# Input projection of a hybrid SSD, attention and PEER layer: 12 of its 30 column chunks multiply in pairs of 512 and 256 columns

## The reference, cut to what matters

```python
xn = rmsnorm(h, norm1_g[i])
proj = xn @ w_in[i]                      # 2048 x (1024 z, 1536 xBC, 16 dt, 1024 q, 128 k, 128 v)
z, xbc, dt_raw, q, k, v = jnp.split(proj, list(IN_SPLITS), axis=-1)
xbc = jax.nn.silu(causal_depthwise_conv(xbc, conv_w[i], conv_b[i]))
...
y_ssd = rmsnorm(ssd_scan(...) * silu(z))
y_att = rmsnorm(swa_sink_attention(q, k, v, attn_sinks[i]))
h = h + concatenate([y_ssd, y_att]) @ w_out[i]
h = h + peer_ffn(rmsnorm(h, norm2_g[i]), ...)      # top-16 of 16384 experts for each of 8 heads
return rmsnorm(h, norm_f_g)
```

## Time and profile before

| | |
|---|---|
| median of 3 runs | 1712.38 us (1712.38 to 1712.72) |
| profiled execution: its time, its span | 1712.57 us, 1710.9 us |
| TensorE busy | 1699.4 us (99% of the span), 9725 matmuls |
| VectorE busy | 1336.6 us (78%) |
| ScalarE busy | 928.2 us (54%) |
| 200 to 210 us (q stage): TensorE, VectorE, ScalarE busy | 10.00, 8.64, 7.89 of 10 us |

### The profile page before, as it was taken

How to read it: one execution, slowest core, us unless ns; L and a number is a source line. 1 busy time by engine, 2 the same in 40 slices (tenths; PEclk the granted TensorE clock), 3 DMA queues, 4 the chain that set the end, 5 groups by cost and what they waited for, 6 DMA issues and landing times.

```text
span 1710.9 us, 26973 instructions
## 1 busy us (share of the span) xinstructions
PE 1699.4 (99%) x9725; PEld 1487.6 (87%) x9725; DVE 1336.6 (78%) x2125; ACT 928.2 (54%) x1593; POOL 547.1 (32%) x337
## 2 busy tenths in 40 slices
PE   9999999999999999999999999999999999999997
PEld 9999998988888888888888888888888888888886
DVE  7888889878999998555555666668878888888887
ACT  7546756544555554554454454465555555555556
POOL 0000000000017787777783000067545422222210
PEclk9999999999999999999999999999999999999999
DMA  7655568776668887778787888899999999999994
GB/s 275 223 196 165 183 198 272 230 240 214 203 197 197 193 197 194 194 198 198 195 192 217 261 266 263 269 364 348 361 340 357 362 364 350 370 359 358 368 335 157
DMA packets 186545, 445.74 MB, mean 261 GB/s; under 512 B 59360, under 2 KB 94448, under 8 KB 177776
## 3 DMA queue, kind: packets, MB, share of 16 engines
q1 hardware_dynamic: 146688, 372.94, 64.6%
q0 software_dynamic: 39504, 71.55, 15.8%
q10 hardware_dynamic: 288, 0.53, 0.1%
HBM read 423.79 MB, written 20.57 MB: 260 GB/s over the span
## 4 chain that ended last, share of the span: by engine, by line
PE 98%; DVE 1%; DMA 0%; issue 0%; ACT 0%; SPq 0%; DVEq 0%
PE ps L1903 23%; PE ps L1909 12%; PE ps L1889 8%; PE ps L2309 7%; PE ps L2311 7%; PE ps L2325 7%; PE ps L2323 7%; PE ps L2321 7%; PE ps L1887 4%; PE ps L1941 3%; PE ps L1942 2%; PE ps L1943 2%; PE ps L2215 2%; PE ps L2131 1%; PE ps L2133 1%; PE ps L2132 1%
## 5 line engine op out<-in xcount | busy, mean ns | idle before, releaser
L1031 DVE TENSOR_TENSOR low<-raw,high 128x1024 fp32r<-128x1024 f32 x376 | 457.9, 1222 | 74.7 <-ACT high L670 64.2
L670 ACT ACTIVATE high<-raw 128x1024 fp32r<-128x1024 f32 x376 | 393.2, 1051 | 53.3 <-PE ps L1943 32.3
L1903 PE MATMUL ps<-acts,high 128*128 128x512 f32 x1472 | 350.5, 390 | 0.0
L1903 PEld LDWEIGHTS ps<-acts,high 128*128 128x128 f32 x1472 | 272.6, 188 | 54.2
L663 ACT ACTIVATE high<-raw 128x1024 fp32r<-128x1024 f32 x172 | 182.5, 1062 | 170.7 <-PE ps L2325 166.6
L621 POOL DMA_INDIRECT big<-v_tab,half_sb x64 | 119.0, 1860 | 477.5 <-DVE big L1775 290.9
L1038 DVE TENSOR_TENSOR low<-raw,high 128x1024 fp32r<-128x1024 f32 x172 | 206.5, 1223 | 62.0 <-ACT high L663 60.8
L601 POOL DMA_INDIRECT gate_scratch<-gates_sb,cells_sb x128 | 214.1, 1673 | 68.8 <-issue 68.8
L929 ACT ACTIVATE side<-ps 128x256 f32<-128x256 f32 x128 | 49.1, 383 | 315.7 <-PE ps L1909 212.7
L1909 PEld LDWEIGHTS ps<-acts,low 128*128 128x128 f32 x1472 | 188.7, 191 | 7.2
L1909 PE MATMUL ps<-acts,low 128*128 128x256 f32 x1472 | 190.9, 283 | 0.0
(11 more groups left out here) (308 smaller groups left out, 3195.4 us busy)
## 6 DMA issues: line engine op xcount, KB each, us to landing
raw<-u_tab SPq DMA_DIRECT2D x256, 512.0 KB
raw<-v_tab SPq DMA_DIRECT2D x172, 512.0 KB
raw_more<-v_tab SPq DMA_DIRECT2D x84, 512.0 KB
raw<-w_in SPq DMA_DIRECT2D x60, 512.0 KB
raw<-w_out SPq DMA_DIRECT2D x32, 512.0 KB
raw<-w_q SPq DMA_DIRECT2D x32, 512.0 KB
gate_scratch<-side SPq DMA_DIRECT2D x32, 384.0 KB, 5.7
big<-gate_scratch SPq DMA_DIRECT2D x16, 768.0 KB, 7.1
```

Source lines behind the costliest of these rows:

```text
L670: nc.scalar.activation(slot(high, s), slot(raw, s), ACT.Copy).then_inc(hi_done, 1)
L1031: V.tensor_tensor(slot(low, s), slot(raw, s), slot(high, s).bitcast(F32), ALU.subtract).then_inc(lo_done, 1)
L1903: mm(both, tile_of(high, kk), both_of(kk), start=(kk == 0), stop=False, skip_group_check=True)
```

## The change

Twelve chunks go over to matmuls in pairs: convolution chunks 10 and 11, keys, values, and the eight of q. Other than `paired_product`, the new `half_pairs` does the eight 512-column matmuls and the eight 256-column ones of one half chunk before it goes to the other half. The takes of these chunks become two VectorE operations with a wait between them: a product of 512 columns out of the bank into a new tile `in_two`, and the sum of its halves. `IN_PAIRED` names chunks 12 and 13 too, which `take_chunk` handles in its other branch.

```diff
+            def take_two(c, bank, dst, r):
+                two = in_two.rearrange("p (s n) -> p s n", s=2)
+                dve.wait_ge(taken, c)
+                dve.wait_ge(used, 2 * c + 2)
+                own.step(V.tensor_tensor(two, ps[:, bank, :].rearrange("p (s n) -> p s n", s=2),
+                                         r.rearrange("p (o n) -> p o n", o=1).broadcast_to([P, 2, T]), ALU.mult))
+                own.settle()
+                V.tensor_tensor(dst, in_two[:, 0:T], in_two[:, T:2 * T], ALU.add).then_inc(taken, 1)
...
+                    if c in IN_PAIRED:
+                        take_two(c, c % 2, conv_in[:, m, CONV_W - 1:CONV_W - 1 + T], rstd1)
+                        return
...
-                    take(c, c % 2, k_t if c == C_K else v_t, rstd1)
+                    take_two(c, c % 2, k_t if c == C_K else v_t, rstd1)
...
-                take(c - 1, (c - 1) % 2, view(QZ + s * T, T), rstd1)
+                take_two(c - 1, (c - 1) % 2, view(QZ + s * T, T), rstd1)
...
+            def half_pairs(c, half, first, last):
+                par = c % 2
+                s = 2 * par + half
+                for k in range(8):
+                    wh = high[:, s * PIECE + k * P:s * PIECE + (k + 1) * P]
+                    mm(ps[:, par, :], wh, both_tiles(8 * half + k), start=first and k == 0, stop=False, skip_group_check=True)
+                for k in range(8):
+                    wl = low[:, s * PIECE + k * P:s * PIECE + (k + 1) * P]
+                    ins = mm(ps[:, par, 0:T], wl, hi_tile(8 * half + k), start=False, stop=last and k == 7,
+                             skip_group_check=True)
+                return ins
+
+            def product_pairs(c):
+                pe.wait_ge(taken, c - 1)
+                for half in range(2):
+                    pe.wait_ge(lo_done, 2 * c + half + 1)
+                    half_pairs(c, half, half == 0, half == 1).then_inc(used, 1)
...
-            product(10, 0)
-            product(11, 1)
-            product(C_K, C_K % 2)
+            product_pairs(10)
+            product_pairs(11)
+            product_pairs(C_K)
...
-            product(C_V, C_V % 2)
+            product_pairs(C_V)
...
-            product(C_Q, C_Q % 2)
+            product_pairs(C_Q)
...
-                part(c, 0, every, acc, normed, True, False).then_inc(used, 1)
+                half_pairs(c, 0, True, False).then_inc(used, 1)
...
-                part(c, 1, every, acc, normed, False, True).then_inc(used, 1)
+                half_pairs(c, 1, False, True).then_inc(used, 1)
```

More of the change, by code:

```diff
@@ L52 @@
 C_WQ = C_OUT + KT
+IN_PAIRED = (10, 11, 12, 13)
 C_U = C_WQ + 2 * PEER_HEADS
@@ L155, in build @@
         sb(ctx, "unused", 2 * KT * T - 2 * DENSE - SPARSE - KT * DENSE - D - 2 * PIECE)
+        with ExitStack() as inputs:
+            in_two = sb(inputs, "in_two", 2 * T)
         with ExitStack() as routing:
@@ L2149, in spread @@
                 ins.then_inc(rows_ok, 1)
-            product(C_Q, C_Q % 2)
+            product_pairs(C_Q)
             pe.wait_ge(y_out, SSD_HEADS)
-            normed, mixed = (hi_tile, lo_tile), (plain(act2_hi), plain(act2_lo))
+            mixed = (plain(act2_hi), plain(act2_lo))
             every = range(8)
@@ L2156, in _ @@
                 c = C_Q + 1 + s
-                acc = ps[:, c % 2, 0:T]
                 pe.wait_ge(taken, c - 1)
                 pe.wait_ge(lo_done, 2 * c + 1)
-                part(c, 0, every, acc, normed, True, False).then_inc(used, 1)
+                half_pairs(c, 0, True, False).then_inc(used, 1)
                 if s:
```

## The result

The changed kernel took **1715.01 us** (median of 20 runs, 1713.76 to 1716.99), the kernel before 1712.58 us beside it (20 runs, 1712.15 to 1714.39): ratio 1.0014, 95% interval 1.0008 to 1.002. So it is 2.4 us slower, less than the 0.2% within which this kernel counts as unchanged, but the interval excludes 1. The forecast was 1715.3, +2.9. The profiled execution is the slowest of the 20 (1716.99 us, span 1715.4).

What follows compares the result with a forecast made beforehand. TensorE fills 98% of the chain, but the q-stage loop through VectorE's longer take was to bind: +0.31 us by chunk 15, growing to +2.9 at the last turn, on the 1712.38 median 1715.3 us, range 1712.6 to 1717.2.

Steps and rivals of the forecast that it cites:

- What TensorE saves: Twelve paired chunks: a half chunk falls from 2.88 to 2.78 us, 2.4 us at most over 24 halves.
- What VectorE pays: Each two-operation take: 0.68 product, 0.03 wait and 0.42 sum replace 0.42, so 0.71 us more.
- Chunks 10 to 13: Convolution, keys and values: takes of 10, 11 and 13 fall in idle time, take 12 does not; TensorE 0.31 us late.
- The stall ahead of chunk 15: TensorE waits 0.95 us for VectorE's low cut, 0.71 late, with the load ahead of it assumed unmoved.
- The restart: TensorE resuming after a wait in mid-stream at chunk 15: costs between nothing and 0.28 us, taken as 0.10.
- The q stage: Loop of logits, maxes, exponentials, shares, take: slack 0.49 to 0.56 us against 0.71 more per take; last turn +2.82, plus 0.04 restart.
- The steps that the forecast called covered, 2 and 4: q stage: longer takes there hidden behind other VectorE work, so no TensorE idle before logits.
- (A): Rival, whole kernel: VectorE's extra stays hidden and the whole 2.4 us is saved, 1710.0 us; chance 5%.
- (B): Rival: only the stall at chunk 15 comes and the q stage keeps its pace, -1.3, 1711.1 us; chance 8%.
- (C): Rival: measurably slower, from 0.78 us extra a take (+3.4) or restarts 0.10 dearer each; chance 27%.

Runs made afterwards that it cites:

- Pairs with the old take: Changed kernel with all pairs on TensorE, but VectorE's one-operation take of the left half, right half left out; -1.93 us against the kernel before, ratio interval 0.9983 to 1.0001.
- second profile of the changed kernel: Profile from running the changed kernel again without edit; that run's median was 1714.84 us against 1712.82 for the kernel before.
- best version: Changed kernel with q takes ahead of shares, keys' take earlier, add_halves of step 0 and a low cut of step 2 behind shares; 1710.98 us against 1712.54.
- the take ahead of shares: Changed kernel with take_two moved from behind shares to ahead of them in each q step; 1712.26 us against 1712.61 for the kernel before.

## Why the prediction was right, point by point

**What TensorE saves.** Right in kind, a little too high in size. A half fell from 2.88 to 2.80 us instead of 2.78, since eight wide matmuls take 1.84 us, 0.230 each and not the 0.228 of the earlier trace rows: 0.083 a half, 2.0 us for 24, not 2.4. Pairs with the old take gave -1.93. The Trainium skill ("TensorE: Matmul & The Clock Gate", Back-to-back issue gap) would have had 0.5 us in all by the formula that the forecast took, 109 and 216 ns; measured are 120 and 230 ns from start to start. The forecast left out that the section gives this formula for an isolated matmul and says that it under-counts at small N and over-counts at large N where each matmul follows a weight load of its own. Here the trace agrees with the first (120 for 109) and not with the second (230 for 216).

**What VectorE pays.** 0.684 + 0.04 + 0.425 - 0.42 = 0.73, forecast 0.71.

**Chunks 10 to 13.** Their takes are covered, as forecast. The stall ahead of chunk 15 is the term with a wrong premise: I held the landing of the load fixed, and it moves by 2.7 us from one execution to the next. TensorE's idle time there was 0.49 in the second profile of the changed kernel, and none is listed in the first (0.06 by the starts), 0.95 forecast. Counted from `cumulate`, chunk 15 started +0.28 late in the second profile (102.05 - 69.37 = 32.68 against 32.40), nearly the +0.21 of the forecast. The idle time is shorter for the same lateness for two reasons. 0.16 more is not listed, since the matmul of 101.28 is shown to 101.56 and the next was due at 101.40: by the starts the wait is 0.65. And TensorE had already waited once before, which the forecast missed: chunk 14 needs the bank that take 12 frees. In the second profile that take ends at 95.06 + 0.43 = 95.49 (VectorE):

```profile
94.35 0.68 DVE L1149 TENSOR_TENSOR in_two<-ps,big 128x512 f32<-128x512 f32 x1
95.06 0.43 DVE L1152 TENSOR_TENSOR big<-in_two 128x256 f32<-128x256 f32 x1
```

and TensorE, whose last eight narrow matmuls from 94.39 need 0.96, goes on at 95.54 and not at 95.35, with 0.23 to the second matmul in place of 0.12, so it loses 0.19 + 0.11 there. With the 0.65 that is 0.95, the forecast's sum, at two places in place of one; less 8 halves of 0.083 it is the +0.28.

```profile
94.39 1.11 PE L1939 MATMUL ps<-acts,low 128*128 128x256 f32 x8
95.54 0.39 PE L1978 MATMUL ps<-acts,high 128*128 128x256 f32 x1
95.77 0.28 PE L1979 MATMUL ps<-acts,high 128*128 128x256 f32 x1
```

In the first profile, with the load 0.9 earlier, that take is done in time, and chunk 15 starts 103.66 - 71.86 = 31.80 from `cumulate`, 0.60 early. The restart cost about what I took: 0.07 more at chunk 15 (0.19 from the first to the second matmul where 0.12 is usual) and 0.11 at chunk 14, against 0.10.

**The q stage.** The forecast shifts against those of the second profile, each less its `cumulate` (0.16 later than before):

| place | forecast | measured |
|---|---|---|
| logits(0) | 0.0 | +0.10 |
| logits(1) | +0.59 | +0.56 |
| logits(3) | +0.83 | +0.73 |
| logits(5) | +1.13 | +1.00 |
| last turn | +2.86 | +2.78 |

The takes between agree as well: the one of step 6 ended +2.04 for +2.11, that of step 7 +2.77 for +2.82. The steps that the forecast called covered, 2 and 4, are the two without a wait; the other five stall 0.39 to 0.41 each. The steps from logits to logits show the two kinds side by side (us):

| step | 0 | 1 | 2 | 3 | 4 | 5 | 6 | 7 (to the last turn) |
|---|---|---|---|---|---|---|---|---|
| before | 7.18 | 8.87 | 7.18 | 8.67 | 7.78 | 7.78 | 8.14 | 6.89 |
| changed, second profile | 7.64 | 8.74 | 7.48 | 8.52 | 8.20 | 8.31 | 8.67 | 7.61 |
| moved takes, best version | 7.16 | 8.73 | 7.03 | 8.85 | 7.74 | 7.64 | 8.07 | 6.89 |

The long steps 1 and 3 fell by 0.13 to 0.15, TensorE's saving; in every other step the loop through VectorE is the longer and the step grew by 0.30 to 0.72. The best version pays in step 3 alone (+0.18, the late turn above) and gains in the rest or stays level. From logits(0) to the last turn the changed kernel needs 65.11 us in the first profile and 65.17 in the second, before 62.49, the best version 62.11.

**Against the rivals.** That the extra stays hidden (A) or that only chunk 15 stalls (B) is ruled out by the run with q only: +2.64, with the same waits in the q stage. The measurable loss (C) did not come: it needed 0.78 more per take or dearer restarts, and 0.73 a take and 0.07 to 0.11 a restart were measured.

**What stays less certain.** The median moved by +2.0 to +2.4, the shift from `cumulate` to the last turn by +2.78 in one profile and +1.85 in the other; these two differ by the stall at chunk 15. The three profiles with the long take of the keys in its old place and the pairs in chunks 10 to 13 that have a late load show it one for one: load at 21.86, 22.04 and 22.74 behind `cumulate`, logits(0) at 88.44, 88.63 and 89.31 (the middle one is the take ahead of shares). Where the load came at 20.4 or 20.9, logits(0) of the pairs stood at 88.30 or 88.31. No run fixed that load, so that it is what spreads the single times is argued and not shown. The total is closer than the shift: 1715.3 for 1715.01, but +2.9 for +2.0 to +2.4, since the kernel before measured 0.2 higher beside the changed one than in the three runs that the sum starts from. And +2.9 was made for an execution with a late load, so that the median came this near is in part luck.

**Pairs with the old take** did not get all of 2.0 us to the last turn (1.55), though no wait of TensorE is listed in the q stage. The 11 halves ahead of logits(0) gave 0.91, all of theirs. From logits(0) to the last turn lie 13 halves, 1.08 us, and the stretch is 0.64 shorter (61.85 for 62.49). Most of the rest is lost in two steps: step 0 falls by only 0.02 where 0.17 was due, and step 7, which has no product of q to shorten, is 0.24 longer. The starts show why. In step 0 the turn is due at 162.85 + 0.96 = 163.81 and starts at 163.89, 0.06 behind the shares (163.14 + 0.69 = 163.83); the logits behind it come after 0.58 in place of 0.53. The last turn is due at 218.80 + 0.12 = 218.92 and starts at 219.16, again 0.06 behind the shares (218.41 + 0.69 = 219.10), which had waited 2.00 for ScalarE's exponentials. So even with the short take these shares don't come as early as TensorE now could use them: the loop's length is the next limit, right behind the saving.

## What to carry to other kernels

When an edit shortens TensorE and lengthens an eviction, ask first what loop the eviction stands in: here 0.73 us on an engine that is busy 78% of the time cost more than 0.083 us a half on the engine that is busy 99% gave back, because next to it the slack was 0.5 us a step. An eviction whose data are ready early belongs in the idle time ahead of a wait, not behind it, and each step has to be looked at by itself: in two of eight that idle time was already taken, and they ate the whole gain of the q stage until two other pieces of work were moved. An order that gives nothing alone can be what makes another change pay.

## What the runs showed of the hardware that was not expected

**A slow start in one execution.** In the first profile of the changed kernel TensorE's first product waits 1.92 us and starts at 9.65; in the kernel before it starts at 7.96 after 1.03. From 10.27 on the matmuls run slower, 0.21 from start to start in place of 0.12:

```profile
9.65 0.39 PE L2067 MATMUL ps<-acts,high 128*128 128x256 f32 x1 [1.92 <-DVE low L1087]
...
10.70 0.41 PE L2067 MATMUL ps<-acts,high 128*128 128x256 f32 x1
10.91 0.41 PE L2068 MATMUL ps<-acts,high 128*128 128x256 f32 x1
```

The windows view of that execution (stretch, us, busy us of PE, PEld, DVE, ACT, POOL, then the granted clock, DMA share and GB/s) has the clock at 0.77 and 0.80, so part of these 8 us at 1.2 instead of 2.4 GHz:

```profile
8.00:12.00 4.00, 2.35 (x13) 2.35 (x14) 2.61 (x5) 2.99 (x6) 0.00 (x0) 0.77 1.03 420
12.00:16.00 4.00, 4.00 (x29) 4.00 (x29) 3.96 (x10) 4.00 (x10) 0.00 (x0) 0.80 0.99 374
```

The same stretch of the kernel before:

```profile
8.00:12.00 4.00, 3.72 (x29) 3.52 (x30) 2.88 (x6) 2.85 (x7) 0.00 (x0) 1.00 1.02 418
```

The late first product is 1.69 of the 2.65 us by which `cumulate` is late; it came with the weights. ScalarE's first high cut waits 2.09 us for the load of `w_in` and starts at 8.24, in the kernel before after 0.34 at 6.55, 1.69 sooner. The other 0.96 is the slower clock: 17 matmuls from 10.11 to 13.65 take 3.54 us in place of 2.04, 1.50 more, of which the kernel before loses 0.54 in the same place to a wait for operands (0.78 from 9.38 to 10.16 where 0.24 is usual). Why that load was late isn't known. The second profile of the same program starts its product at 8.37 and has `cumulate` at 69.37, so it is no property of the change. The spans of the two first profiles alone, 1715.4 against 1710.9, would have said 4.5 us.

**A load that lands anywhere within 2.7 us.** The cut that waits for the same load, issued at the same place of the program, started 20.4 to 23.1 us behind `cumulate` in twelve profiles, and 22.77 and 22.00 in two of one program. A stall forecast from one profile, behind a transfer with that spread, is a stall of that execution.
